# First attention: value products turned over on two column halves, scores two units ahead, probability copies by ScalarE and VectorE in turn

## The chip, the cores and the metric

The kernel runs on one core of one Trainium2 chip. Its engines work from queues of their own and meet in semaphores: TensorE (PE; its weight loads are listed apart as PEld), VectorE (DVE), ScalarE (ACT), GpSimd (POOL) and SyncE (SP), which here issues the loads and stores. The metric is the device time of one execution in microseconds, from start to end of the program; lower is better.

## What is computed

One inference step of a two-layer decoder for 1024 prompt tokens and 8 sample tokens, 1032 columns in all. The change lies in the prompt part of the first layer's latent attention (16 heads):

```python
def mla_prompt_attn(q_nope, q_rope, ckv, k_rope, w_uk, w_uv):
    k_nope = jnp.einsum('nsc,chd->nshd', ckv, w_uk)
    v = jnp.einsum('nsc,chd->nshd', ckv, w_uv)
    ...
    def block(args):
        i, qn_b, qr_b = args
        s = (jnp.einsum('nqhd,nshd->nhqs', qn_b, k_nope)
             + jnp.einsum('nqhr,nsr->nhqs', qr_b, k_rope)).astype(jnp.float32) * MLA_SCALE
        qpos = i * Q_BLOCK + jnp.arange(Q_BLOCK)
        s = jnp.where(kpos[None, :] <= qpos[:, None], s, NEG)
        p = jax.nn.softmax(s, axis=-1).astype(v.dtype)
        return jnp.einsum('nhqs,nshd->nqhd', p, v)
```

A head has 64 plain and 32 rotated query and key columns and 64 value columns. All is float32.

## The kernel before

Activations lie with channels on the partitions and tokens in the columns. The stage is a loop over four groups of four heads (`gi`). In a group TensorE first projects: two tiles of plain queries (L911), a tile of the rotary parts of four heads, keys (L918), the rotary tile with its halves swapped by a product with a permutation matrix (`swap16`, L926), keys again, values (L940). ScalarE and VectorE copy the results out of PSUM and VectorE applies the rotation (L1076 to L1081).

Then come 32 units (`UNITS`): a unit is one head and one block of 128 queries. Causality gives query block `qb` only `qb`+1 key blocks, so units take the blocks in the order 0, 7, 1, 6, 2, 5, 3, 4, each for the two heads of a pair in turn. A unit goes through these steps, each a wait on a semaphore of the step before:

- `scores(u)` on TensorE (L953): queries by up to 1024 keys, into one of two areas of two PSUM banks, by turns.
- `maximum(u)` on VectorE (L1096 to L1098): the causal mask is added to the diagonal block, the row maximum taken and scaled.
- `exponential(u)` on ScalarE (L1022): exp with the row sum beside it, into `prob` in SBUF.
- `turn(u)` on TensorE (L964): the probabilities are transposed block by block, four to a PSUM bank (a batch), by turns into bank 4 and bank 5.
- `turned(u)`: ScalarE copies the even batches out (L1034), VectorE the odd ones (L1119), into `probT`.
- `values(u)` on TensorE (L976): for each key block the transposed probabilities, 128x128, are the stationary side and the 64 value columns of the head stream; the sum is 128 queries by 64.
- `normalise(u)` on VectorE (L1104, L1108): the reciprocal of the row sum, and the product by it, into `onat`.
- `turn_out(pr)` on TensorE (L984) transposes the 128x128 result of a pair of heads, and `outputs(pr)` copies it to `mixa`, on ScalarE (L1041) or VectorE (L1126).

The order on each engine is written out by hand. TensorE's loop over `u` issues `scores(u+1)`, `values(u-1)`, `turn(u)` and, after every second unit, `turn_out`. VectorE's issues `maximum(u+1)`, `normalise(u-1)`, `turned(u)`, `outputs`; ScalarE's `exponential(u+1)`, `turned(u)`, `outputs`. A float32 product is two TensorE instructions in the trace, a transposition one.

After the stage comes decode over the paged cache (L1220 on), whose weights `wukT`, `wuv` and `sel` SP loads behind this stage's weights. Two later places show forms that this stage does not have yet: in decode, products on four 32-column quarters of the array (L1263, L1279), and in the second layer's attention, products on two 64-column halves (L1891) and a lane shuffle on VectorE (L1782).

## Time and profile before

| | us |
|---|---|
| median of 3 runs | 3428.65 |
| lowest and highest | 3427.99, 3432.38 |
| the profiled execution | 3433.76 |
| its span, first to last instruction | 3431.9 |
| TensorE busy in the span | 3109.9 (91%) |
| VectorE busy | 1806.9 (53%) |
| ScalarE busy | 692.1 (20%) |
| GpSimd busy | 881.0 (26%) |
| this stage, first projection to the end of the last output copy | 340.0 to 909.1 |

Durations come from one profiled execution. Matmuls are pipelined, and each is listed with its way through the array, so the pace of a run of matmuls is read from its start to the start of the next, or as the run's length less one tail. In the stage view the columns are the stretch, its length, the busy time and number of instructions of PE, PEld, DVE, ACT and POOL, the granted clock of TensorE as a share of 2.4 GHz, the share of the DMA engines and GB/s. In the timeline they are start, length, engine, line, operation, output and inputs, shapes, number of instructions, and in brackets the idle time before with what ended it.

### The profile page before, as it was taken

What the parts mean: (1) busy time and instruction counts of PE and PEld (TensorE: products, weight loads), DVE (VectorE), ACT (ScalarE), POOL (GpSimd) and SP (SyncE); (2) the same over time, 40 slices, a digit from 0 to 9 for tenths busy, and PEclk for the clock granted to TensorE, in tenths of its full rate; (3) what the DMA queues carried; (4) which work ended last, traced back from release to release, by engine and by line L of the source; (5) the groups of instructions that cost most, each with busy time, mean ns of one, the idle gap of its engine ahead of it and who ended that gap; (6) DMA issues with size and microseconds to landing.
All of it is one profiled execution on the core that took longest, in us unless ns stands there. A gap on an engine that the chain in (4) does not pass through costs nothing. (4 is left out here: it accounts for less than half of the span.)

```text
span 3431.9 us, 58662 instructions
## 1 busy us (share of the span) xinstructions
PE 3109.9 (91%) x21903; PEld 2787.8 (81%) x21903; DVE 1806.9 (53%) x2943; ACT 692.1 (20%) x1446; POOL 881.0 (26%) x496
## 2 busy tenths in 40 slices
PE   6865888888888887999999999998979999999996
PEld 6843666666666666999999999997559999999996
DVE  8694555555455554375253434565865533525354
ACT  3101333333233332021000000100742100000001
POOL 3200000000011111443443434442015344443432
PEclk9887999999899998999999999999989999999998
DMA  2101000100166663111111111122111111111112
GB/s 95 50 1 41 14 1 13 38 0 0 56 194 194 197 192 118 46 55 45 54 43 44 49 43 51 42 64 64 50 53 57 47 43 49 43 49 42 50 42 71
DMA packets 129123, 205.77 MB, mean 60 GB/s; under 512 B 14833, under 2 KB 95729, under 8 KB 128274
## 3 DMA queue, kind: packets, MB, share of 16 engines
q1 hardware_dynamic: 127858, 200.07, 19.1%
q10 hardware_dynamic: 1152, 4.23, 0.3%
q8 instruction: 67, 1.10, 0.1%
q14 instruction: 46, 0.38, 0.0%
HBM read 189.87 MB, written 6.25 MB: 57 GB/s over the span
## 5 line engine op out<-in xcount | busy, mean ns | idle before, releaser
L137 PE MATMUL ps_trunk_out<-sb_h_hi,sb_slab_hi 128*128 128x344 f32 x2400 | 768.0, 320 | 0.0
L138 PE MATMUL ps_trunk_out<-sb_h_hi,sb_slab_lo 128*128 128x344 f32 x2400 | 764.8, 319 | 0.0
L139 PE MATMUL ps_trunk_out<-sb_h_lo,sb_slab_hi 128*128 128x344 f32 x2400 | 764.4, 319 | 0.0
L121 POOL TENSOR_TENSOR sb_slab_hi<-sb_slab_raw,sb_ones 128x1024 fp32r<-128x1024 f32 (+3 forms) x214 | 345.7, 1615 | 1367.0 <-PE ps_trunk_out L139 1051.8
L123 POOL TENSOR_TENSOR sb_slab_lo<-sb_slab_raw,sb_slab_hi 128x1024 fp32r<-128x1024 f32 (+3 forms) x214 | 488.6, 2283 | 16.8
L138 PEld LDWEIGHTS ps_trunk_out<-sb_h_hi,sb_slab_lo 128*128 128x128 f32 x2400 | 450.4, 188 | 0.6
L137 PEld LDWEIGHTS ps_trunk_out<-sb_h_hi,sb_slab_hi 128*128 128x128 f32 x2400 | 450.4, 188 | 0.6
L139 PEld LDWEIGHTS ps_trunk_out<-sb_h_lo,sb_slab_hi 128*128 128x128 f32 x2400 | 450.4, 188 | 0.0
L137 PE MATMUL ps_trunk_out<-sb_ffn_a_hi,sb_slab_hi 128*128 128x344 f32 x1056 | 336.9, 319 | 4.9 <-DVEq L1601 4.9
L139 PE MATMUL ps_trunk_out<-sb_ffn_a_lo,sb_slab_hi 128*128 128x344 f32 x1056 | 337.9, 320 | 0.0
L138 PE MATMUL ps_trunk_out<-sb_ffn_a_hi,sb_slab_lo 128*128 128x344 f32 x1056 | 336.2, 318 | 0.0
L1329 POOL TENSOR_TENSOR sb_dec_kr<-sb_dec_ck,sb_ones 128x256 f32<-128x256 f32 x64 | 46.7, 729 | 1127.6 <-DMA sb_dec_ck<-cache 1030.1
L1554 ACT ACTIVATE sb_ffn_a<-sb_ffn_c 128x1032 f32<-128x1032 f32 x44 | 47.0, 1067 | 995.5 <-DVEq L1591 995.5
L976 PEld LDWEIGHTS ps_mla_bank<-sb_mla_v,sb_mla_probT 128*128 128x128 f32 x1152 | 146.0, 196 | 88.2 <-ACT sb_mla_probT L1034 68.1
L1610 DVE TENSOR_TENSOR sb_z<-sb_z,ps_trunk_out 128x1032 f32 x48 | 59.0, 1229 | 300.5 <-PE ps_trunk_out L139 300.5
L137 PEld LDWEIGHTS ps_trunk_out<-sb_ffn_a_hi,sb_slab_hi 128*128 128x128 f32 x1056 | 198.4, 188 | 6.0 <-DVEq L1601 6.0
L139 PEld LDWEIGHTS ps_trunk_out<-sb_ffn_a_lo,sb_slab_hi 128*128 128x128 f32 x1056 | 198.5, 188 | 0.0
L138 PEld LDWEIGHTS ps_trunk_out<-sb_ffn_a_hi,sb_slab_lo 128*128 128x128 f32 x1056 | 198.4, 188 | 0.0
L976 PE MATMUL ps_mla_bank<-sb_mla_v,sb_mla_probT 128*128 128x64 f32 x1152 | 152.8, 279 | 39.3 <-ACT sb_mla_probT L1034 38.9
L1578 DVE TENSOR_TENSOR sb_ffn_g<-ps_trunk_out,sb_rstd 128x1032 f32<-128x1032 f32 x44 | 54.2, 1233 | 230.6 <-PE ps_trunk_out L139 230.6
L953 PE MATMUL ps_mla_bank<-sb_mla_k,sb_mla_q 96*128 96x512 f32 (+3 forms) x384 | 157.3, 522 | 2.7 <-ACT sb_mla_v L1015 2.7
L1022 ACT ACTIVATE sb_mla_prob<-ps_mla_bank,sb_mla_nmx 128x1024 f32<-128x1024 f32 (+7 forms) x128 | 94.9, 741 | 208.5 <-DVE sb_mla_nmx L1098 191.2
(393 smaller groups left out, 5168.2 us busy)
## 6 DMA issues: line engine op xcount, KB each, us to landing
sb_dec_ck<-cache SPq DMA_DIRECT2D x512, 144.0 KB, 2.4
sb_slab_raw<-f_w_gu SPq DMA_DIRECT2D x88, 512.0 KB, 3.5
sb_slab_raw<-f_w_down SPq DMA_DIRECT2D x32, 384.0 KB, 3.1
sb_slab_raw<-f_w_down SPq DMA_DIRECT2D x32, 320.0 KB, 2.8
sb_slab_raw<-e_w_out SPq DMA_DIRECT2D x24, 256.0 KB, 2.6
sb_slab_raw<-o_w_in SPq DMA_DIRECT2D x12, 512.0 KB, 3.5
sb_slab_raw<-e_w_in SPq DMA_DIRECT2D x10, 512.0 KB, 3.2
sb_x_first<-x SPq DMA_DIRECT2D x8, 516.0 KB, 8.5
```

The source lines that it names most:

```text
L121: nc.gpsimd.tensor_tensor(hi, raw, one, ALU.mult).then_inc(self.hi_done[s], 1)
L123: nc.gpsimd.tensor_tensor(self.lo[:, s, 0:kc, :], raw, hi.bitcast(F32), ALU.subtract).then_inc(self.split_done[s], 1)
L137: nc.tensor.matmul(out[:, t, 0:TT], a, x_hi(k)[:, cols], start=k == 0, stop=False)
L138: nc.tensor.matmul(out[:, t, 0:TT], b, x_hi(k)[:, cols], start=False, stop=False)
L139: last = nc.tensor.matmul(out[:, t, 0:TT], a, x_lo(k)[:, cols], start=False, stop=k == kc - 1)
L953: m = MM(bank[:, 2 * (u % 2) + c0 // 512, 0:c1 - c0], qg[:, h, qb * P:(qb + 1) * P], kg[:, h, c0:c1], start=True, stop=True)
L976: m = MM(bank[:, 6 + u % 2, 0:DV], probT[:, u % 2, kb, :], vg[:, kb, h * DV:(h + 1) * DV], start=kb == 0, stop=kb == qb)
L1022: nc.scalar.activation(prob[:, u % 2, 0:(qb + 1) * P], bank[:, 2 * (u % 2):2 * (u % 2) + 2, :].rearrange("p a b -> p (a b)")[:, 0:(qb + 1) ...
L1329: nc.gpsimd.tensor_tensor(kr[:, c % 2], ck[:, c % SLOTS, :, KVL:CW], one, ALU.mult).then_inc(kr_done, 1)
L1554: nc.scalar.activation(a[:, :], c[:, :], ACT.Gelu_apprx_tanh).then_inc(ffn_act_done, 1)
L1578: ch.link(V.tensor_tensor(v3(g[:, 2:]), slabs.out[:, 0, :, 0:TT], v3(rstd), ALU.mult))
L1610: V.tensor_tensor(xm, xm, slabs.out[:, s, :, 0:TT], ALU.add).then_inc(slabs.free[s], 1)
```

## The change

- Projections: the rotary tile is projected first. The swap of its halves is a `stream_shuffle` on VectorE instead of the product with `swap16`; `ra` and `rb` lie in two tiles of `z`. Key and value projections go to other banks. The decode weights on SP wait until VectorE has ended the fourth group's projections.
- Units: four units form a quad: small block, large block, for head 0, then the same for head 1 ((0,7), (1,6), (2,5), (3,4)). Small scores have bank 4, large ones banks 0 and 1 or 2 and 3. `prob` and `probT` are doubled.
- TensorE issues `scores(u+2)`, `turn(u)`, and, twice per quad, `values(pr)` for a pair of heads: the value columns are stationary and the transposed probabilities stream, head 0 on array columns 0 to 63 and head 1 on 64 to 127. The result is already turned. A second product, ones by `diag`, spreads the inverse row sums over the partitions.
- VectorE takes one reciprocal per pair; GpSimd makes `diag`, the identity times the inverse sums. `outputs` on VectorE copies the spread sums to `over` and multiplies the result by them into `mixa`. `normalise`, `turn_out` and the copies after it go.
- Batches are numbered so that a large unit's two batches go to ScalarE and VectorE one each, and the small units' by turns.

```diff
+            prob = [sb("mla_prob_s", [P, 2, 512]), sb("mla_prob_l", [P, 2, T])]
+            probT = [sb("mla_probT_s", [P, 2, 2, 4, P]), sb("mla_probT_l", [P, 2, 2, QB, P])]
+            mx, nmx = sb("mla_mx", [P, 4]), sb("mla_nmx", [P, 4])
+            rs, rinv, diag = sb("mla_rs", [P, 2, 4]), sb("mla_rinv", [P, 4]), sb("mla_diag", [P, 2, 2, P])
+            over = sb("mla_over", [P, 1, P])
...
+            def unit(u):
+                qd, big, hh = u // 4, u % 2, u // 2 % 2
+                qb = ((0, 7), (1, 6), (2, 5), (3, 4))[qd % 4][big]
+                return qd, big, hh, qb, 2 * (qd // 4) + hh
+            def batches(u):
+                qd, big, hh, qb, _ = unit(u)
+                b = 6 * qd + 3 * hh + big
+                return [(b + j, 4 * j, min(4, qb + 1 - 4 * j)) for j in range(1 + big)]
+            def score(u):
+                _, big, hh, qb, _ = unit(u)
+                s = bank[:, 2 * hh:2 * hh + 2, :].rearrange("p a b -> p (a b)") if big else bank[:, 4, :]
+                return s[:, 0:(qb + 1) * P]
...
+                    sp.wait_ge(dve_ev, 4 * 5)
                     sp.dma_start(wukT[:, :, :], A["w_ukT"]).then_inc(dec_w_in, 16)
...
+                @block.gpsimd
+                def _(pool):
+                    with pool.Fori(0, 4) as gi:
+                        for pr in range(NPAIR):
+                            big = pr % 2
+                            pool.wait_ge(rinv_done, gi * NPAIR + (pr + 1))
+                            nc.gpsimd.tensor_tensor(diag[:, big], ident[:, :].unsqueeze(1).broadcast_to((P, 2, P)),
+                                                    rinv[:, 2 * big:2 * big + 2].unsqueeze(2).broadcast_to((P, 2, P)),
+                                                    ALU.mult).then_inc(diag_done, 1)
...
+                        pe.wait_ge(w_in, gi * 32 + 32)
+                        pe.wait_ge(exp_done, gi * UNITS + 1)
+                        queries(2, 0)
+                        for e in t_ev:
+                            pe.wait_ge(e, gi * (NB // 2) + 1)
+                        queries(0, 3)
+                        pe.wait_ge(act_ev, gi * 5 + 1)
+                        queries(1, 0)
+                        pe.wait_ge(o_done, gi * NPAIR + 1)
+                        keys(0, 6)
...
-                        for t in range(3):
-                            m = MM(bank[:, t, 0:TT], swap16[:, :], qraw[:, t * TT:(t + 1) * TT], start=True, stop=True)
-                        m.then_inc(proj, 1)
...
+                        keys(1, 3)
+                        for v, b0 in enumerate((5, 6, 7, 0)):
...
+                        def scores(u):
+                            qd, big, hh, qb, h = unit(u)
+                            if big and u >= 4:
+                                pe.wait_ge(exp_done, gi * UNITS + (u - 2))
+                            elif not big and u >= 2:
+                                pe.wait_ge(exp_done, gi * UNITS + u)
+                            for c0 in range(0, (qb + 1) * P, 512):
+                                c1 = min((qb + 1) * P, c0 + 512)
+                                m = MM(score(u)[:, c0:c1], qg[:, h, qb * P:(qb + 1) * P], kg[:, h, c0:c1], start=True, stop=True)
...
+                        def turn(u):
+                            qd, big, hh, qb, h = unit(u)
+                            pe.wait_ge(exp_done, gi * UNITS + (u + 2))
+                            for b, b0, nb in batches(u):
+                                if b >= 2:
+                                    pe.wait_ge(t_ev[b % 2], gi * (NB // 2) + (b // 2 + 1))
+                                for q in range(nb):
+                                    m = nc.tensor.transpose(bank[:, 5 + b % 2, q * P:(q + 1) * P],
+                                                            prob[big][:, hh, (b0 + q) * P:(b0 + q + 1) * P], ident[:, :])
+                                m.then_inc(t_done, 1)
+                        def values(pr):
+                            u = last_of(pr)
+                            qd, big, _, qb, h = unit(u)
+                            for e in range(2):
+                                pe.wait_ge(t_ev[e], gi * (NB // 2) + (3 * qd + (4 if big else 2 + e)))
+                            pe.wait_ge(o_done, gi * NPAIR + (pr + 1))
+                            for kb in range(qb + 1):
+                                for hh in range(2):
+                                    MM(bank[hh * DV:(hh + 1) * DV, 7, big * 256:big * 256 + P],
+                                       vg[:, kb, (h - 1 + hh) * DV:(h + hh) * DV], probT[big][:, qd % 2, hh, kb, :],
+                                       start=kb == 0, stop=kb == qb)
+                            pe.wait_ge(diag_done, gi * NPAIR + (pr + 1))
+                            for hh in range(2):
+                                m = MM(bank[hh * DV:(hh + 1) * DV, 7, big * 256 + P:big * 256 + 2 * P], ones[:, 0:DV],
+                                       diag[:, big, hh, :], start=True, stop=True)
+                            m.then_inc(pv_done, 1)
+                        pe.wait_ge(act_ev, gi * 5 + 3)
+                        scores(0)
...
-                        for u in range(UNITS + 2):
-                            if u + 1 < UNITS:
-                                scores(u + 1)
-                            if 1 <= u <= UNITS:
-                                values(u - 1)
+                        for u in range(UNITS + 1):
+                            if u + 2 < UNITS:
+                                scores(u + 2)
                             if u < UNITS:
                                 turn(u)
-                            if u >= 3 and u % 2 == 1:
-                                turn_out((u - 3) // 2)
+                            if u >= 3 and u % 4 in (3, 0):
+                                values((u - 3) // 4 * 2 + (u % 4 == 0))
...
+                            if u >= 4:
+                                act.wait_ge(t_done, gi * NB + (batches(u - 4)[-1][0] + 1))
+                            nc.scalar.activation(prob[big][:, hh, 0:(qb + 1) * P], score(u), ACT.Exp, scale=MLA_SCALE,
+                                                 bias=nmx[:, u % 4:u % 4 + 1],
+                                                 accum_out=rs[:, qd % 2, 2 * big + hh:2 * big + hh + 1]).then_inc(exp_done, 1)
...
                                 act.wait_ge(t_done, gi * NB + (b + 1))
-                                nc.scalar.copy(mixa[:, bass.ds(gi * 2 + hp, 1), qb * P:(qb + 1) * P],
-                                               bank[:, 4:5, 0:P]).then_inc(ta_ev, 1)
+                                nc.scalar.copy(probT[big][:, qd % 2, hh, b0:b0 + nb, :],
+                                               bank[:, 5 + b % 2, 0:nb * P].rearrange("p (a b) -> p a b", b=P)).then_inc(t_ev[0], 1)
...
+                        dve.wait_ge(act_ev, gi * 5 + 1)
+                        V.tensor_tensor(ra, qraw[:, :], rot[:, 0, :], ALU.mult)
+                        ch.link(V.stream_shuffle(rb, qraw[:, :], swap_lanes))
+                        ch.link(V.tensor_tensor(rb, rb, rot[:, 1, :], ALU.mult))
...
+                        def inverse(pr):
+                            big = pr % 2
+                            dve.wait_ge(exp_done, gi * UNITS + (last_of(pr) + 2))
+                            V.reciprocal(rinv[:, 2 * big:2 * big + 2],
+                                         rs[:, pr // 2 % 2, 2 * big:2 * big + 2]).then_inc(rinv_done, 1)
...
+                                if b % 2:
+                                    dve.wait_ge(t_done, gi * NB + (b + 1))
+                                    V.tensor_copy(probT[big][:, qd % 2, hh, b0:b0 + nb, :],
+                                                  bank[:, 6, 0:nb * P].rearrange("p (a b) -> p a b", b=P)).then_inc(t_ev[1], 1)
+                        def outputs(pr):
+                            qd, big, _, qb, _ = unit(last_of(pr))
+                            dve.wait_ge(pv_done, gi * NPAIR + (pr + 1))
+                            ch.link(V.tensor_copy(over[:, 0, :], bank[:, 7, big * 256 + P:big * 256 + 2 * P]))
+                            V.tensor_tensor(mixa[:, bass.ds(gi * 2 + qd // 4, 1), qb * P:(qb + 1) * P],
+                                            bank[:, 7:8, big * 256:big * 256 + P], over[:, :, :], ALU.mult).then_inc(o_done, 1)
...
-                            if u + 1 < UNITS:
-                                maximum(u + 1)
-                            if 1 <= u <= UNITS:
-                                normalise(u - 1)
+                            if u >= 4 and u % 4 in (0, 1):
+                                outputs((u - 4) // 4 * 2 + u % 4)
+                            if u + 2 < UNITS:
+                                maximum(u + 2)
+                            if u < UNITS and u % 4 >= 2:
+                                inverse(u // 4 * 2 + u % 4 - 2)
                             if u < UNITS:
                                 turned(u)
-                            if u >= 3 and u % 2 == 1:
-                                outputs((u - 3) // 2)
```

## Rows read from the trace of the kernel before

**Rows 1.** The page's head.

```profile
span 3431.9 us, 58662 instructions
```

**Rows 2.** Stages: length, busy PE, PEld, DVE, ACT, POOL; granted clock.

```profile
340.00:909.10 569.10, 495.71 (x2608) 353.14 (x2608) 305.66 (x820) 187.03 (x415) 0.00 (x0) 0.95 0.03 10
...
481.80:517.80 36.00, 33.59 (x108) 21.11 (x108) 13.74 (x13) 6.24 (x7) 0.00 (x0) 0.95 0.00 0
...
935.00:1320.00 385.00, 337.61 (x4590) 258.81 (x4590) 220.34 (x642) 144.84 (x412) 45.20 (x62) 0.99 0.64 184
...
2436.00:2533.00 97.00, 86.52 (x598) 53.05 (x598) 82.39 (x250) 65.48 (x247) 0.00 (x0) 1.00 0.17 55
```

**Rows 3.** Waits from 377 to 909 us: total us, times, longest.

```profile
PE ps_mla_bank L976 <- ACT sb_mla_probT L1034: 38.9, 52, 2.1
...
PE ps_mla_bank L984 <- ACT sb_mla_probT L1034: 15.3, 30, 0.7
...
DVE sb_mla_onat L1108 <- PE ps_mla_bank L976: 44.0, 56, 2.3
```

**Rows 4.** Timeline of group 1: start us, length, engine, what.

```profile
418.77 1.45 PE L976 MATMUL ps_mla_bank<-sb_mla_v,sb_mla_probT 128*128 128x64 f32 x12
...
418.98 0.30 DVE L1096 TENSOR_TENSOR ps_mla_bank<-ps_mla_bank,sb_mla_mask 128x128 f32<-128x128 f32 x1 [1.31 <-PE ps_mla_bank L953]
...
433.25 1.88 PE L953 MATMUL ps_mla_bank<-sb_mla_k,sb_mla_q 96*128 96x512 f32 x4
...
434.92 1.11 ACT L1022 ACTIVATE sb_mla_prob<-ps_mla_bank,sb_mla_nmx 128x1024 f32<-128x1024 f32 x1 [3.37 <-DVE sb_mla_nmx L1098]
...
436.50 0.91 PEld L964 LDWEIGHTS ps_mla_bank<-sb_ident,sb_mla_prob 128*128 128x128 f32 x8
```

**Rows 5.** VectorE's groups by shape, 377 to 909 us: busy, mean, idle.

```profile
L1096 DVE TENSOR_TENSOR ps_mla_bank<-ps_mla_bank,sb_mla_mask 128x128 f32<-128x128 f32 x128 | 38.1, 297 | 81.9 <-PE ps_mla_bank L953 81.2
...
L1108 DVE TENSOR_SCALAR sb_mla_onat<-ps_mla_bank,sb_mla_rinv 128x64 f32<-128x64 f32 x128 | 36.3, 284 | 63.6 <-PE ps_mla_bank L976 44.0 <-issue 14.2
...
L1098 DVE TENSOR_SCALAR sb_mla_nmx<-sb_mla_mx 128x1 f32<-128x1 f32 x128 | 19.6, 153 | 4.4
...
L1097 DVE TENSOR_REDUCE sb_mla_mx<-ps_mla_bank 128x1 f32<-128x1024 f32 x16 | 19.6, 1224 | 0.5
...
L1097 DVE TENSOR_REDUCE sb_mla_mx<-ps_mla_bank 128x1 f32<-128x128 f32 x16 | 4.7, 291 | 0.5
...
L1119 DVE COPY sb_mla_probT<-ps_mla_bank 128x512 f32<-128x512 f32 x24 | 16.5, 690 | 7.2 <-PE ps_mla_bank L964 5.9
```

**Rows 6.** Timeline of the second layer's attention: products on two column halves.

```profile
2445.79 0.63 PEld L1891 LDWEIGHTS ps_swa_bank<-sb_swa_probT,sb_swa_v 128*64 128x64 f32 x8 [0.17 <-issue]
...
2446.80 0.30 PEld L1866 LDWEIGHTS ps_swa_bank<-sb_swa_mask_r,sb_ident_r 128*128 128x128 f32 x2 [0.39 <-issue]
```

**Rows 7.** Timeline of decode, weight loads: four column quarters.

```profile
1119.27 0.30 PEld L1260 LDWEIGHTS ps_dec_bank<-sb_dec_kT,sb_dec_qd 128*128 128x128 f32 x2 [0.41 <-issue]
...
1119.69 0.40 PEld L1263 LDWEIGHTS ps_dec_bank<-sb_dec_cT,sb_dec_qc 128*32 128x32 f32 x16
...
1120.28 0.20 PEld L1246 LDWEIGHTS ps_dec_bank<-sb_ident,sb_dec_kr 128*128 128x128 f32 x2 [0.20 <-issue]
```

**Rows 8.** Timeline of the decode stage, GpSimd beside VectorE.

```profile
1138.87 0.73 POOL L1329 TENSOR_TENSOR sb_dec_kr<-sb_dec_ck,sb_ones 128x256 f32<-128x256 f32 x1 [5.83 <-DMA sb_dec_ck<-cache]
...
1138.96 0.66 DVE L1420 TENSOR_TENSOR sb_dec_mnew<-sb_dec_cmax,sb_dec_m 128x1 f32<-128x1 f32 x1
```

**Rows 9.** Timeline of group 2's projections, TensorE.

```profile
502.62 1.90 PE L926 MATMUL ps_mla_bank<-sb_mla_qraw,sb_swap 128*128 128x344 f32 x6
...
505.33 3.70 PE L918 MATMUL ps_mla_bank<-sb_z,sb_mla_wkv 128*128 128x512 f32 x8 [0.81 <-DVE sb_mla_k L1073]
...
513.42 3.72 PE L940 MATMUL ps_mla_bank<-sb_mla_wkv,sb_z 128*128 128x256 f32 x16 [0.93 <-DVE sb_mla_v L1085]
```

**Rows 10.** VectorE's groups by line, whole span: the shuffle.

```profile
L1782 DVE STREAM_SHUFFLE sb_swa_zs<-sb_z 128x1032 f32<-128x1032 f32 x10 | 13.4, 1340 | 0.1
```

More of the change, by code:

```diff
@@ L901, in _, with queries @@
                     with pe.Fori(0, 4) as gi:
-                        pe.wait_ge(w_in, gi * 32 + 32)
-                        for e in (ta_ev, td_ev):
-                            pe.wait_ge(e, gi * (NB // 2) + 1)
-                        for tile, b0, (s, w) in ((0, 0, (None, 0)), (1, 3, (None, 0)), (2, 0, (act_ev, 1))):
-                            if s is not None:
-                                pe.wait_ge(s, gi * 5 + w)
+                        def queries(tile, b0):
                             for t in range(3):
@@ L946, in scores @@
                         def scores(u):
-                            hp, qb, hh = units[u]
-                            h, n = 2 * hp + hh, (qb + 1) * P
-                            if u >= 2:
-                                pe.wait_ge(exp_done, gi * UNITS + (u - 1))
-                            for c0 in range(0, n, 512):
-                                c1 = min(n, c0 + 512)
-                                m = MM(bank[:, 2 * (u % 2) + c0 // 512, 0:c1 - c0], qg[:, h, qb * P:(qb + 1) * P],
-                                       kg[:, h, c0:c1], start=True, stop=True)
+                            qd, big, hh, qb, h = unit(u)
@@ L987, in _ @@
-                        scores(0)
-                        for u in range(UNITS + 2):
-                            if u + 1 < UNITS:
-                                scores(u + 1)
-                            if 1 <= u <= UNITS:
-                                values(u - 1)
+                        pe.wait_ge(act_ev, gi * 5 + 3)
+                        scores(0)
+                        pe.wait_ge(act_ev, gi * 5 + 5)
+                        scores(1)
+                        pe.wait_ge(dve_ev, gi * 5 + 5)
@@ L1012, in _ @@
                         m.then_inc(act_ev, 1)
-                        for v in (1, 3):
-                            act.wait_ge(proj, gi * NPROJ + (8 + v))
-                            nc.scalar.copy(vg[:, 2 * v:2 * v + 2, :], v2(bank[:, 7, :])).then_inc(act_ev, 1)
+                        for v, b0 in ((1, 6), (3, 0)):
+                            act.wait_ge(proj, gi * NPROJ + (7 + v))
+                            nc.scalar.copy(vg[:, 2 * v:2 * v + 2, :], split2(bank[:, b0, :])).then_inc(act_ev, 1)
@@ L1037, in outputs @@
-                        def outputs(pr):
-                            (hp, qb, _), b = units[2 * pr], of_pair(pr)
-                            if b % 2 == 0:
+                            if u >= 4:
[3 more added lines that the diff above has]
+                                                 accum_out=rs[:, qd % 2, 2 * big + hh:2 * big + hh + 1]).then_inc(exp_done, 1)
@@ L1044, in _ @@
                         exponential(0)
-                        for u in range(UNITS + 2):
+                        for u in range(UNITS):
                             if u + 1 < UNITS:
                                 exponential(u + 1)
-                            if u < UNITS:
-                                turned(u)
-                            if u >= 3 and u % 2 == 1:
-                                outputs((u - 3) // 2)
+                            turned(u)
                 @block.vector
@@ new lines, in _ @@
+                        m.then_inc(dve_ev, 1)
+                        dve.wait_ge(proj, gi * NPROJ + 5)
+                        for hh in range(2):
+                            m = V.tensor_copy(split2(kg[0:NOPE, hh, :]), bank[hh * NOPE:(hh + 1) * NOPE, 6:8, :])
+                        m.then_inc(dve_ev, 1)
+                        for v, b0 in ((0, 5), (2, 7)):
+                            dve.wait_ge(proj, gi * NPROJ + (7 + v))
+                            V.tensor_copy(vg[:, 2 * v:2 * v + 2, :], split2(bank[:, b0, :])).then_inc(dve_ev, 1)
@@ new lines, in maximum @@
+                        def maximum(u):
+                            qd, big, hh, qb, _ = unit(u)
+                            s, c = score(u), slice(u % 4, u % 4 + 1)
+                            block_ = s[:, qb * P:(qb + 1) * P]
+                            dve.wait_ge(s_done, gi * UNITS + (u + 1))
+                            ch.link(V.tensor_tensor(block_, block_, mask[:, 1, :], ALU.add))
+                            ch.link(V.tensor_reduce(mx[:, c], s, AX, ALU.max))
+                            V.tensor_scalar(nmx[:, c], mx[:, c], -MLA_SCALE, None, ALU.mult).then_inc(mx_done, 1)
@@ L1087, in _ @@
+                        maximum(0)
+                        dve.wait_ge(act_ev, gi * 5 + 2)
                         dve.wait_ge(dve_ev, gi * 5 + 5)
                         V.tensor_copy(qs[:, bass.ds(gi * HG, HG), :], qg[:, :, T:NT]).then_inc(qs_done, 1)
-                        def maximum(u):
-                            hp, qb, hh = units[u]
-                            s = bank[:, 2 * (u % 2):2 * (u % 2) + 2, :].rearrange("p a b -> p (a b)")
-                            diag = s[:, qb * P:(qb + 1) * P]
-                            c = slice(u % 4, u % 4 + 1)
-                            dve.wait_ge(s_done, gi * UNITS + (u + 1))
-                            ch.link(V.tensor_tensor(diag, diag, mask[:, 1, :], ALU.add))
-                            ch.link(V.tensor_reduce(mx[:, c], s[:, 0:(qb + 1) * P], AX, ALU.max))
-                            V.tensor_scalar(nmx[:, c], mx[:, c], -MLA_SCALE, None, ALU.mult).then_inc(mx_done, 1)
```

160 lines of the change are left out of this document (38 added, 122 removed).

## The prediction

> **What bounds the kernel now.** I read the stage view first. The diff touches one stage, the first layer's prompt attention, which runs from 340.0 to 909.1 us of a span of 3431.9 us [rows 1, 2]: 569.1 us, four equal groups of 142.3 us, each with 36.0 us of projections and 106.3 us of attention. TensorE is the engine to look at: 495.7 of 569.1 us busy against 305.7 on VectorE and 187.0 on ScalarE. A busy TensorE is not a full one, so I read the pace from the timeline. At the full 2.4 GHz a score product of 1024 keys (four instructions) takes 1.88 us with its tail, so 0.213 us per 128 keys; twelve instructions of the value products take 1.45 us, so 0.119 us each; eight transposes load in 0.91 us, so 0.117 us each with the step to the next [rows 4]. One group has 144 key blocks (each of four heads has 36), so scores cost 144 x 0.213 = 30.7 us, transposes 144 x 0.117 = 16.9 us, values 288 instructions x 0.119 = 34.3 us, and the 16 transposes of outputs 1.9 us: 83.8 us of the 106.3. The rest is in the wait view: TensorE stands before the value products and before the output transposes for ScalarE's copies, 38.9 + 15.3 us, with smaller ones about 66 us over the four groups, or 16.5 per group [rows 3]. 83.8 + 16.5 is 100.3; the granted clock of 0.95 over the stage [rows 2] (a tenth of the time at 1.2 GHz) makes up the other 5 or so. So the stage is TensorE's own pace plus a round trip through the other engines in each unit.
>
> **The value products.** Now the transposed probabilities (128 columns) are the stationary side and 64 value columns stream; the weight load sets the 0.119 us. After, 64 value columns are stationary and the probabilities stream, 128 columns, with heads 0 and 1 of a pair on the two column halves. Instructions per key block stay two. What one costs depends on whether the halves run side by side. Rows of such products stand in this trace: in the second layer eight instructions of 256 columns on two halves take 1.01 us from first load to the next line's first load, 0.17 us of it a gap, so 0.107 us each, half of the 0.213 us that 256 columns take alone [rows 4, 6]. In decode sixteen of 128 columns on four quarters need 0.59 us with 0.20 us of gap, 0.025 us each, a quarter [rows 7]. Mine are 128 columns on two halves: 0.107/2 = 0.053, taken as 0.055 us. Bounds: 0.053 from below, 0.107 (no overlap) from above; I take the low end because both neighbours overlap fully. Each block of value products also switches the array twice. The rows show 0.17 us going in and 0.2 to 0.4 us of loader idling going out, 0.17 us of it lost [rows 6, 7]; I charge 0.30 us per block.
>
> The Trainium skill, "TensorEngine Tiling (Array Packing)", Key Properties, says that changing the tiling mode drains the engine; it gives no figure. The gaps of rows 6 and 7 agree. By a reading without that rule the sum would be 16 x 0.30 x 4 = 19 us lower.
>
> **The division.** The row scaling (128 x 284 ns on VectorE [rows 5]), 64 output transposes and the 64 copies after them go. In their place, per pair of heads: one reciprocal instead of two, a GpSimd product of 128x256, four TensorE instructions that spread the inverse sums (0.22 us), and on VectorE a copy and a product of 128x128 out of PSUM, 0.29 and 0.30 us by the nearest forms [rows 5], 0.65 us with the step between. A block for n key blocks on TensorE is then V(n) = 0.22n + 0.52 us. The GpSimd product is 0.73 us for the same size [rows 8]; it starts at least 1.5 us before TensorE asks for it, so it costs nothing; it would have to take about 3 us to count. Beside such a product VectorE's operation of one column on two SBUF tensors took 0.66 us [rows 8] (0.15 us for a one-column operation with no product beside it [rows 5]); the loop has no VectorE operation with two SBUF tensors, so I charge 0 (upper bound: 0.5 us x 64 = 32 us).
>
> **The order.** Scores are now issued two units ahead, small and large query blocks alternate with three score areas, so TensorE no longer waits for the maximum and exponential of the unit just scored. Per quad (two blocks, two heads, nine key blocks per head) TensorE's work is 3.84 (scores) + 2.1 (transposes) + 0.22 x 9 + 1.04 (values) = 9.0 us, VectorE's about 8.3 us: 4 x (0.30 + 0.15) masks and scalings, 3.03 reductions, 1.67 copies, 1.3 outputs, steps. Both nearly equal, so I walked the queues of one quad with these prices: M(n) = 0.67 + 0.133n for a maximum (from the two reductions, 291 and 1224 ns), 0.69 us for a copy of four blocks, 1.1 us + 0.1 for the widest exponential, 0.2 us from a product to its reader (the next line's matmul starts at 418.77, the mask addition at 418.98) [rows 4, 5]. Two stalls stay. (a) The first half of head 0's large transposes is copied by VectorE, but queued behind the maximum of the next large unit; the next small unit's transposes need that buffer. With the end of the large score product at 0, the maximum ends at 0.2 + 1.74, the copy at 2.62; TensorE has work only until 1.36: 1.3 us lost. (b) The large block's value products wait for the copy of the second half, behind another maximum, and for the small block's outputs: 7.57 us against 6.62 us, 0.9 us lost. The walk for the four kinds of quad, us from the end of the current large scores:
>
> | blocks, then next | first-half copy | small transposes | next large scores | large transposes | small values | second copy | outputs | large values | end |
> |---|---|---|---|---|---|---|---|---|---|
> | 1+8, 2+7 | 2.62 | 2.8 | 4.3 | 5.2 | 6.0 | 6.9 | 7.5 | 9.85 | 11.3 |
> | 2+7, 3+6 | 2.49 | 2.8 | 4.05 | 4.9 | 5.8 | 6.4 | 7.0 | 9.1 | 10.4 |
> | 3+6, 4+5 | 2.36 | 2.8 | 3.8 | 4.5 | 5.7 | 6.1 | 6.7 | 8.9 | 9.9 |
> | 4+5, 1+8 | 2.22 | 2.7 | 4.4 | 5.0 | 6.4 | 6.8 | 7.4 | 9.1 | 10.8 |
>
> Each column ends where its engine and its wait allow. Seven steps from quad to quad sum to 74.2 us. The start costs 5.2 us: small score 0.2, value copy 0.6, large 1.7, small 0.2, large 1.7, and 0.5 as the second maximum is still running. The end is 7.7 us: 3.8 until the last transpose, 1.4 and 1.6 for the values, 0.9 for the outputs between them. Attention is 87.1 us per group at full clock, against 100.3 by the same prices now.
>
> **The projections.** The swap product goes, 1.72 us per group (1.90 with its tail), and a shuffle of 1.34 us on VectorE comes [rows 9, 10]. The rotary tile comes first, so the 8.7 us of VectorE's rotary work run under the next two query tiles (2 x 5.16 us); VectorE is free for its copies at 15.7 us, when the third tile is ready. Keys and values get other banks: the waits of 0.81 + 0.93 us (1.0 + 1.1 at the loader) go [rows 9], and the last shrinks by 0.5. 36.0 - 1.7 - 2.1 - 0.5 = 31.7 us; 0.6 of that last wait is already in the 5.2 above, so 31.1. If VectorE is late there, up to the same 2.1 us comes back. The three weight loads for decode now wait until VectorE has ended group 4's projections, some 85 us before decode reads them; nothing but they are queued behind that on SP. Cost 0. ScalarE keeps its load within a few us and waits most of the time.
>
> **The sum.** Per group 31.1 + 87.1 = 118.2 us; for TensorE's share at the lower clock I add 3.5 us to the attention (4.5% of its 72 us; the projections' 36.0 holds its own): 121.7. Four groups and 0.9 us for the last outputs: 487.7 against 569.1 us, 81.4 less. The profiled execution took 3433.8 us; 3352.4 is its forecast. The median of the runs is 3428.65, 5.1 us lower, so I predict 3347.3 us.
>
> **The rivals.**
> - The two stalls vanish, because VectorE's queue turns faster than I walked it (its copies overlap by 0.08 us each) and TensorE runs at its own pace: 1.6 us x 32 quads = 51 us more, 3296. For it: the engines' sums allow it. Against: the copy behind the maximum is in program order, and that chain has no slack. 0.10.
> - VectorE becomes the bound: each of its steps waits longer than walked, 1.5 us more per quad, 48 us: 3395. For it: 8.3 of 10.6 us of a quad is VectorE work, and all four chains cross it. 0.14. The Trainium skill's same page, PSUM Bottleneck, warns that a faster array leaves the copies out of PSUM as the limit; its reading is this rival, and the VectorE sum above agrees that it is near.
> - The halves do not overlap with 128 streaming columns: 0.107 instead of 0.055 us. After what the stalls hide, 13.6 us per group return, 54 in all: 3401. Rows 6 and 7 speak against it. 0.08.
> - The change does not do what it says: the scores are not ahead in effect, TensorE still waits 16.5 us per group; what stays is 83.8 - 71.9 (9.0 x 8) = 11.9 us and the projections' 4.3, 65 us: 3364, inside the main case.
> - Slower: the granted clock. If half-array products with the stalls between let the clock fall to 1.2 GHz, TensorE's 72 us of attention per group take twice that at worst: +288 us, 3635. It turns the sign once a further 28% of that work runs at the low level. Against: the clock was 0.99 in decode and 1.00 in the second layer's attention, both with column tiles [rows 2]; stalls here are of the length of those now. 0.04.
> - Same as before within 0.2% (which is about what a measurement of this kernel can tell from no change): several of these at once. 0.02.
>
> **How the numbers follow.** Forecast 0.62, 3347.3, its own range 3322 to 3375 (stall prices off by a third either way, and the 0.5 us per GpSimd product as far as it would fall on the path). The range wanted holds eight in ten: from 3305, short of the first rival, to 3398, which takes in the VectorE rival and most of the shared-port bound. Faster by over 0.2%: 0.94; within: 0.02; slower: 0.04.
>
> **What would show it.** Stage about 488 us. L1096's mask additions start 0.2 us after the score products, with TensorE idle mainly before small units' transposes and before the large block's value products, released by VectorE copies. Value product loads 0.055 us apart. Head 0's first-half copy of a large unit follows the maximum. GpSimd busy about 47 us more, no wait on it. I am wrong if the value instructions stand 0.1 us apart, if the clock in the stage falls under 0.9, or if the idle time ahead of the transposes is absent or double.

## The result and the profile after

The changed kernel takes 3338.18 us (median of 4 runs, 3337.84 to 3343.56); the kernel before takes 3428.32 us beside it. The ratio is 0.9742, with a 95% interval of 0.9729 to 0.9756: 2.6% faster. The forecast was 3347.3 us, 9.1 us too slow, inside its own narrow range of 3322 to 3375.

First the page's head after and the lines that answer to the table of before: TensorE is busy 75 us less, VectorE 7 us and ScalarE 9 us less, GpSimd 39 us more.

```profile
span 3336.0 us, 58640 instructions
## 1 busy us (share of the span) xinstructions
PE 3034.9 (91%) x22071; PEld 2720.9 (82%) x22071; DVE 1800.3 (54%) x2855; ACT 682.9 (20%) x1414; POOL 920.4 (28%) x560
```

The stage view of after, the answer to [rows 2]: group 1, group 2's projections and the stage; group 2's attention stands with the experiment on the look-ahead (length, busy PE, PEld, DVE, ACT, POOL, then the granted clock as the third number from the end).

```profile
339.70:459.90 120.20, 107.79 (x695) 72.56 (x695) 73.77 (x181) 45.02 (x96) 9.80 (x16) 0.96 0.03 10
459.90:489.40 29.50, 29.50 (x105) 19.56 (x104) 15.47 (x16) 5.64 (x6) 0.00 (x0) 1.00 0.00 1
...
339.70:812.40 472.70, 420.12 (x2776) 284.22 (x2776) 296.84 (x732) 178.31 (x383) 39.19 (x64) 0.98 0.04 12
```

The stage went from 569.1 to 472.7 us, 96.4 less; the span fell by 95.9, so all of the gain is here. TensorE starts a group's projections at 339.7, 459.9, 576.4 and 692.9 us, so the groups take 120.2, 116.5, 116.5 and 119.5 us, against 142.3 before. In group 2, 29.5 us are projections, with TensorE busy throughout, where they were 36.0. Group 1's projections follow a wait of 13.0 us for the weights and have a granted clock of 0.91, those of the other groups 1.00.

The waits of after in the stage, the answer to [rows 3] (engine, line, releaser: total us, times, longest; PE first, then its loader, then VectorE):

```profile
PE ps_mla_bank L976 <- DVE sb_mla_probT_l L1109: 34.6, 32, 1.6
...
PE ps_mla_bank L988 <- DVE sb_mixa L1116: 9.9, 15, 0.8
PE ps_mla_bank L976 <- ACT sb_mla_prob_l L1034: 4.1, 4, 1.0
...
PEld ps_mla_bank L988 <- DVE sb_mixa L1116: 15.7, 24, 1.2
...
DVE ps_mla_bank L1092 <- PE ps_mla_bank L966: 50.9, 64, 1.3
```

The old waits for ScalarE's copies, 38.9 + 15.3 us, are gone. In their place stand the two stalls of the forecast: 32 waits of 1.08 us (one in each of 32 quads) before a small unit's transposes, released by VectorE's first-half copy (a), and a shorter one before the large block's value products, released by VectorE's outputs (b).

One quad in the timeline of after (start us, length, engine, line, what). It shows the turned-over products and both stalls.

```profile
384.33 0.29 DVE L1116 TENSOR_TENSOR sb_mixa<-ps_mla_bank,sb_mla_over 128x128 f32 x1 [0.16 <-DVE sb_mla_over L1115]
...
384.68 1.73 PEld L988 LDWEIGHTS ps_mla_bank<-sb_mla_probT_l,sb_mla_v 128*64 128x64 f32 x32 [0.94 <-DVE sb_mixa L1116]
...
386.37 0.25 PEld L993 LDWEIGHTS ps_mla_bank<-sb_mla_diag,sb_ones 128*64 128x64 f32 x4
...
386.80 0.30 PEld L966 LDWEIGHTS ps_mla_bank<-sb_mla_k,sb_mla_q 96*128 96x128 f32 x2 [0.17 <-issue]
386.80 1.77 PE L966 MATMUL ps_mla_bank<-sb_mla_k,sb_mla_q 96*128 96x512 f32 x4
...
388.61 0.30 DVE L1092 TENSOR_TENSOR ps_mla_bank<-ps_mla_bank,sb_mla_mask 128x128 f32<-128x128 f32 x1 [0.95 <-PE ps_mla_bank L966]
388.94 1.09 DVE L1093 TENSOR_REDUCE sb_mla_mx<-ps_mla_bank 128x1 f32<-128x896 f32 x1
...
390.16 0.69 DVE L1109 COPY sb_mla_probT_l<-ps_mla_bank 128x512 f32<-128x512 f32 x1
...
391.00 0.41 PE L976 MATMUL ps_mla_bank<-sb_ident,sb_mla_prob_s 128*128 128x128 f32 x2 [1.02 <-DVE sb_mla_probT_l L1109]
```

The 32 loads of the large block run from 384.68 to the next line's first load at 386.37, 0.053 us apart: the pace at which two halves side by side had been priced. The array's switch is the gap of 0.17 us ahead of L966. Stall (a) is in the last four lines: all transposes of the large unit have been in PSUM since 389.3, but VectorE first does the mask (388.61) and the maximum (388.94) of the next large unit, copies at 390.16, and TensorE starts its next transposes at 391.00.

### The profile page after: what moved, and what is told of

The parts are those of the page before. It is cut to its first block and busy times, and to the rows that moved or that the text cites. A ratio compares the mean times of both kernels' runs of the same rounds, so it can differ in the third digit from the quotient of the medians.

```text
span 3336.0 us, 58640 instructions
## 1 busy us (share of the span) xinstructions
PE 3034.9 (91%) x22071; PEld 2720.9 (82%) x22071; DVE 1800.3 (54%) x2855; ACT 682.9 (20%) x1414; POOL 920.4 (28%) x560
## 5 line engine op out<-in xcount | busy, mean ns | idle before, releaser
L913 POOL TENSOR_TENSOR sb_mla_diag<-sb_ident,sb_mla_rinv 128x256 f32<-128x256 f32 x64 | 39.2, 612 | 632.3 <-DVE sb_mla_rinv L1099 632.3
L966 PE MATMUL ps_mla_bank<-sb_mla_k,sb_mla_q 96*128 96x512 f32 (+3 forms) x384 | 150.7, 503 | 1.8 <-ACT sb_mla_v L1027 1.8
L1235 PE MATMUL ps_dec_bank<-sb_ident,sb_dec_ck 128*128 128x128 f32 x1024 | 134.3, 275 | 0.0
L1582 DVE TENSOR_TENSOR sb_ffn_u<-sb_rstd,ps_trunk_out 128x1032 f32<-128x1032 f32 x44 | 54.1, 1230 | 135.3 <-PE ps_trunk_out L139 135.0
```

Source lines behind the costliest of these rows:

```text
L966: m = MM(score(u)[:, c0:c1], qg[:, h, qb * P:(qb + 1) * P], kg[:, h, c0:c1], start=True, stop=True)
L1235: m = nc.tensor.transpose(bank[:, b % 4, k * P:(k + 1) * P], src, ident[:, :])
L1582: ch.link(V.tensor_tensor(v3(u[:, :]), v3(rstd), slabs.out[:, 1, :, 0:TT], ALU.mult))
```

## The experiments

All have the changed kernel as their base, and each ratio is to the kernel before on the same chip. The runs of before scatter by up to 7 us either way, so I read differences from the changed kernel's 3338.2 us in medians, beside the ratio. Where a few us matter I compare the attention of one group at a granted clock of 1.00 in both kernels: it is 87.0 us in the changed kernel (group 2).

**Do the halves run side by side?**

```diff
-for kb in range(qb + 1):
-    for hh in range(2):
+for hh in range(2):
+    for kb in range(qb + 1):
         MM(bank[hh * DV:(hh + 1) * DV, 7, ...
```

> Head 1's value products come after all of head 0's, each still on its own column half, so no two neighbours lie on different halves. Same instructions, same count. Theory (the halves run side by side): a value load stands 0.107 instead of 0.053 us from the next, and 54 us come back: about 3392 us. Rival (a 64-column load alone gives the pace of 0.053 us, neighbours don't matter): unchanged, 3338 us.

3372.47 us, ratio 0.9823 (0.9807 to 0.984): 34 us slower. Its loads in the same large block:

```profile
384.28 2.87 PEld L988 LDWEIGHTS ps_mla_bank<-sb_mla_probT_l,sb_mla_v 128*64 128x64 f32 x30 [0.94 <-DVE sb_mixa L1116]
```

30 loads in 2.87 us, the last one's own 0.14 us taken off, are 0.094 us apart; the same reading of the changed kernel (1.73 us, 32 loads) gives 0.051. The same instructions on the same halves, only in another order, take 1.8 times as long, so the pace comes from neighbours on different halves. The rival of an unchanged time falls. The size was wrong, 34 us where the expectation had 54: a load takes 0.094, not 0.107 us, the change of heads inside a block keeps its short step, and with one key block the order of heads changes nothing (four loads of 0.20 us in both). The stalls did not hide any of it: the sums of the two waits are the same 34.6 and 10.0 us, and TensorE's idle time in group 2's attention is 13.0 us against 13.1.

**Stall (a): is it the copy's place in VectorE's queue?** The first kernel moves one copy per quad to ScalarE (the edit below, shortened; each copy still raises the semaphore of its batch), the second moves them all.

```diff
 for b, b0, nb in batches(u):      # ScalarE
-    if b % 2:
+    if b % 2 and b % 6 != 1:
         continue
...
-    if b % 2:                     # VectorE
+    if b % 2 and b % 6 != 1:
```

> One copy per quad moved from VectorE to ScalarE: the first half of head 0's large transposes, the one that stands behind the maximum (stall a). Theory (this queue position is what TensorE waits for): the 34.6 us of TensorE's waits for it go, and VectorE has 0.69 us less to do in each of 32 quads: 30 to 42 us faster than the changed kernel, about 3300 us. Rival (the sum of VectorE's work is what bounds, and only its 22 us less count): about 3316 us. Rival (the wait only moves to the next one): 3333 to 3338 us.

> All copies of transposed probabilities on ScalarE, none on VectorE. Theory (both stalls come from copies queued behind a maximum on VectorE): the walk of a quad with 1+8 blocks gives 9.6 instead of 11.3 us; over 32 quads about 48 us less than the changed kernel, 3290 us. Rival (ScalarE, with exponentials and all copies in one queue, becomes the late one): the stall of the first half is replaced by one before the transposes, 3320 us or more.

The first took 3307.68 us, ratio 0.9635 (0.9619 to 0.9652): 30.5 us faster than the changed kernel. All copies on ScalarE took 3297.62 us, ratio 0.9615 (0.9599 to 0.9631): 40.6 us faster. TensorE's waits of the first, then of the second (same view as above):

```profile
PE ps_mla_bank L988 <- DVE sb_mixa L1116: 9.0, 16, 0.8
PE ps_mla_bank L976 <- ACT sb_mla_prob_l L1034: 7.7, 12, 1.0
PE ps_mla_bank L976 <- ACT sb_mla_probT_l L1046: 4.4, 8, 0.7
```

```profile
PE ps_mla_bank L976 <- ACT sb_mla_prob_l L1034: 6.5, 8, 1.0
PE ps_mla_bank L988 <- DVE sb_mixa L1114: 4.5, 8, 0.8
PE ps_mla_bank L976 <- ACT sb_mla_probT_l L1044: 4.4, 8, 0.7
```

Moving one copy of 0.69 us takes 34.6 us of waits down to 4.4 and leaves (b) nearly as it was; 3.6 us move to the waits for the exponential (4.1 to 7.7). 30.5 us come off the time. At a clock of 1.00 the attention of a group falls from 87.0 to 79.9 us, 28.6 us over four groups; the other 2 us are no more than the clock costs the changed kernel in the attention of groups 1 and 4 (3 us). VectorE's whole queue as the bound would have given 22. Moving the rest halves (b) and gives 10 us more. The two stalls together are worth 41 us where the walk had 48 to 51. ScalarE has room: in group 2 of the second kernel it is busy 52.8 us of 107.5. The Trainium skill, "TensorEngine Tiling (Array Packing)", PSUM Bottleneck, advises the use of both ScalarE and VectorE to empty PSUM; by that the changed kernel's split should be the better one. Here the measurement decides against it by 41 us: VectorE's queue also holds the maxima, and a copy behind one holds up TensorE. This version beats both kernels.

**What the look-ahead is worth.**

```diff
-if u + 2 < UNITS:
-    scores(u + 2)       # VectorE: maximum(u + 2)
+if u + 1 < UNITS:
+    scores(u + 1)       # VectorE: maximum(u + 1)
```

> Scores and maximum are issued only one unit ahead instead of two; all else as changed. Theory (the look-ahead is what hides the chain score, maximum, exponential): a large unit's chain is 0.2 + 1.7 + 1.1 = 3.0 us, the TensorE work behind it about 1 us, so up to 2 us per large unit, 128 in all, less what the present stalls already hold (up to 70): 3400 to 3470 us. Rival (as in the prediction, the scores not being ahead costs only the old waits): about 3364 us or less.

3426.97 us, ratio 0.9989 (0.9975 to 1.0003). One unit less of look-ahead gives back 89 us, nearly the whole gain, and the time is inside the first theory's range. The rival, which is the prediction's "the scores are not ahead in effect", falls: it had 3364. The waits, and the stage view of group 2's attention in this kernel and in the changed one:

```profile
PE ps_mla_bank L976 <- ACT sb_mla_prob_l L1033: 73.7, 40, 2.7
```

```profile
510.56:623.82 113.26, 92.56 (x593) 62.14 (x591) 60.07 (x167) 37.83 (x90) 9.80 (x16) 0.82 0.03 10
```

```profile
489.40:576.42 87.02, 73.90 (x594) 50.43 (x592) 58.70 (x167) 39.21 (x90) 9.80 (x16) 1.00 0.04 13
```

Of the 26.2 us that this attention is longer, TensorE's idle time is only 7.6 (20.7 against 13.1). The other 18.7 is busy time for the same instructions: the granted clock stands at 0.82 instead of 1.00 (0.85 or 0.86 in the other three groups), so part of them ran at 1.2 GHz. Over the four attentions idle time grows by 32 us and busy time by 59. My expectation had only waits, up to 2 us for each large unit, so its range was met for the wrong reason.

**Stall (b): are VectorE's outputs on the path?**

```diff
-ch.link(V.tensor_copy(over[:, 0, :], bank[:, 7, big * 256 + P:big * 256 + 2 * P]))
...
-    bank[:, 7:8, big * 256:big * 256 + P], over[:, :, :], ALU.mult)
+    bank[:, 7:8, big * 256:big * 256 + P], ones[:, :].unsqueeze(1), ALU.mult)
```

> Leaves out VectorE's copy of the spread inverse sums, and with it the division: the output product multiplies by ones. 64 copies of 0.29 us and the step of 0.16 us behind each go from VectorE; TensorE does all it did. Theory (stall b: the large block's value products wait for the small block's outputs): 0.45 us per quad, 14 us faster than the changed kernel, 3324 us. Rival (VectorE's whole queue is the bound): 0.45 us x 64 = 29 us faster, 3309 us. Rival (the outputs are off the path): 3338 us.

3326.77 us, ratio 0.9702 (0.9686 to 0.9718): 11.4 us faster, nearest to the 14 us of the first theory. The wait of stall (b), 9.9 us in the changed kernel, is now:

```profile
PE ps_mla_bank L988 <- DVE sb_mixa L1115: 4.0, 12, 0.5
```

The small block's outputs are on the path once per quad; VectorE's sum is not the bound (29 us), and they are not off the path either.

**GpSimd's product: how long may it take?** The next two kernels widen it (the cut edit below; VectorE's reciprocal writes its two values three times for it); the second also runs it twice in a chain.

```diff
-nc.gpsimd.tensor_tensor(diag[:, big], ... (P, 2, P) ..., ALU.mult).then_inc(diag_done, 1)
+nc.gpsimd.tensor_tensor(diag[:, big], ... (P, 6, P) ..., ALU.mult).then_inc(diag_done, 1)
```

> GpSimd's product is three times as wide (128x768 instead of 128x256; TensorE reads the first third), so at most 1.84 us instead of 0.61. Theory (hidden: in the changed kernel TensorE asks 1.3 us after it in a small block and 2.3 us after it in a large one): within 5 us of the changed kernel, 3338. Rival (a longer GpSimd product holds up VectorE, as the one-column operation of 0.66 us seemed to say): 0.2 to 0.5 us per product, 13 to 32 us slower, 3351 to 3370 us, with VectorE's operations visibly longer.

> Two such wide products one after the other, at most 3.7 us. Theory (the slack is 1.3 us in small blocks and 2.3 in large ones, so 1.9 and 2.9 us are the longest that stay hidden): 1.8 us late in a small and 0.8 us in a large block, 26 to 83 us slower over 32 quads, 3364 to 3421 us, and TensorE waits for GpSimd before the four products of the sums. Rival (slack is larger than it looks): 3338 us.

The single wide product took 3338.30 us, ratio 0.9734 (0.9718 to 0.9751), the two in a chain 3370.68 us, ratio 0.9827 (0.9811 to 0.9843). Groups by shape of the single wide product, then one wait of the double one:

```profile
L913 POOL TENSOR_TENSOR sb_mla_diag<-sb_ident,sb_mla_rinv 128x768 f32<-128x768 f32 x64 | 94.1, 1471 | 580.1 <-DVE sb_mla_rinv L1099 579.9
L1092 DVE TENSOR_TENSOR ps_mla_bank<-ps_mla_bank,sb_mla_mask 128x128 f32<-128x128 f32 x128 | 37.9, 296 | 51.8 <-PE ps_mla_bank L966 50.8
L1094 DVE TENSOR_SCALAR sb_mla_nmx<-sb_mla_mx 128x1 f32<-128x1 f32 x128 | 19.6, 153 | 4.4
```

```profile
PE ps_mla_bank L997 <- POOL sb_mla_diag L917: 30.7, 35, 1.2
```

1.47 us cost nothing, and VectorE's masks and scalings keep their mean of 296 and 153 ns (297 and 153 before, [rows 5]). Two such products, 3.0 us, cost 32 us and make 30.7 us of waits, nearly all in the small blocks: 1.1 us late in each of 32 by a limit of 1.9 us is 35. The range was met only because it was wide; I had taken 1.84 us for a product, where it is 1.47. No VectorE operation in this loop has two inputs in SBUF, so what such a one would lose beside GpSimd is not tried here.

**What a switch of the array's mode costs.** One more product between the value products and those of the sums, on the full array or on one half:

```diff
+MM(bank[:, 7, big * 256 + P:big * 256 + 2 * P], ident[:, :], ident[:, :], ...)      # full array
...
+MM(bank[0:DV, 7, big * 256 + P:big * 256 + 2 * P], ident[:, 0:DV], ident[:, :], ...)  # one half
```

> One more full-array product (identity by identity, 128 columns, two instructions) between the value products and the products of the sums, so two more switches of the array's mode per block, 128 in all; its result is overwritten. Theory (a switch costs the 0.17 us gap each way): 64 x (0.21 + 0.34) = 35 us slower, 3373 us. Rival (switches are free, the gaps are something else): 64 x 0.21 = 13 us, 3351 us.

> The same extra product (two instructions, 128 columns) but on one column half, between products that lie on column halves too: no further switch. Theory: 64 x 0.11 to 0.21 = 7 to 14 us slower than the changed kernel, 3345 to 3352 us, and about 22 us faster than the kernel with the full-array product. Rival (the switches are free): both kernels within 7 us of each other.

The full-array product took 3367.32 us, ratio 0.9817 (0.9801 to 0.9833), the half-array one 3352.50 us, ratio 0.9775 (0.9759 to 0.9792): 29 and 14 us over the changed kernel. The large block's loads, full array first:

```profile
383.49 1.73 PEld L988 LDWEIGHTS ps_mla_bank<-sb_mla_probT_l,sb_mla_v 128*64 128x64 f32 x32 [0.37 <-DVE sb_mixa L1117]
385.39 0.30 PEld L991 LDWEIGHTS ps_mla_bank<-sb_ident 128*128 128x128 f32 x2 [0.17 <-issue]
385.80 0.20 PEld L994 LDWEIGHTS ps_mla_bank<-sb_mla_diag,sb_ones 128*64 128x64 f32 x4
386.17 0.30 PEld L966 LDWEIGHTS ps_mla_bank<-sb_mla_k,sb_mla_q 96*128 96x128 f32 x2 [0.17 <-issue]
```

```profile
385.22 1.73 PEld L988 LDWEIGHTS ps_mla_bank<-sb_mla_probT_l,sb_mla_v 128*64 128x64 f32 x32 [0.73 <-DVE sb_mixa L1117]
386.91 0.25 PEld L991 LDWEIGHTS ps_mla_bank<-sb_ident 128*64 128x64 f32 x2
387.02 0.35 PEld L994 LDWEIGHTS ps_mla_bank<-sb_mla_diag,sb_ones 128*64 128x64 f32 x4
387.55 0.30 PEld L966 LDWEIGHTS ps_mla_bank<-sb_mla_k,sb_mla_q 96*128 96x128 f32 x2 [0.17 <-issue]
```

From the first load of L988 to the first of L966 the block takes 2.68 us with the full-array product, 2.33 with the half-array one and 2.12 in the changed kernel (384.68 to 386.80). So the product costs 0.21 us either way, and two switches 0.35 us on top, 0.17 each: the gap is the cost. The expectations had 35 us for the first kernel, 7 to 14 for the second and 22 between them. In the medians only 15 of those 22 show. The wait for VectorE ahead of the block shrinks (0.37 us against 0.73): a group's attention at a clock of 1.00 is 94.8 us against 89.8, 20 us over four groups. Some 2 us more are the clock, for which the half-array kernel paid 6 us (two groups at 0.97 and 0.95) and the other 4 (0.98 and 0.96); the last 3 us are within the scatter of the medians. The rival of free switches, within 7 us, falls.

**Do TensorE's waits bring the clock down?** GpSimd's wide product three times in a chain.

> Three of the wide GpSimd products in a chain (one takes 1.47 us, so 4.5 us; TensorE reads the last): 2.6 us late in a small and 1.6 us in a large block by the slack of 1.9 and 2.9 us. The question is TensorE's clock. With one unit of look-ahead TensorE waited up to 2.7 us at a time and its clock in the attention was 0.82; with two products here it waited up to 1.2 us more and the clock held 0.99. Theory (waits of more than 2 us in each quad bring the clock down): waits of 4.2 us per quad make 134 us, some of it in place of the present stalls (70), and a clock near 0.85 adds some 50 us: 3450 to 3510 us. Rival (the clock holds at 0.97 or more, what brought it down was something else in that kernel): 3400 to 3470 us, and products of values keep 0.053 us in each block.

3493.37 us, ratio 1.0188 (1.0169 to 1.0207), inside the first theory's range and outside the rival's. Group 2's attention with two such products, and with three:

```profile
496.87:592.91 96.04, 77.29 (x594) 51.28 (x592) 59.81 (x168) 39.47 (x90) 46.75 (x32) 0.98 0.03 12
```

```profile
525.25:651.51 126.26, 95.37 (x593) 63.60 (x591) 59.73 (x167) 39.30 (x90) 70.23 (x48) 0.82 0.03 9
```

```profile
PE ps_mla_bank L1001 <- POOL sb_mla_diag L921: 83.4, 41, 2.7
```

TensorE does the same work in both. With waits of up to 1.2 us for GpSimd and 1.6 us for VectorE the clock is 0.98 in this group and 1.00 in the other three; with waits of up to 2.7 us it is 0.82 (0.86 in group 1), as with one unit of look-ahead, though scores are two ahead here. Against the changed kernel this attention is 39.2 us longer: 17.8 idle and 21.5 busy. With two products at a clock of 1.00 TensorE was busy 76.0 us, 2.1 more than in the changed kernel, so some 19 of the 21.5 are the clock. Over four groups that is 73 us idle and 78 busy, where the theory had priced the clock at 50.

It is not TensorE's idle time in total: with one unit of look-ahead a group's attention has 20.7 us of it at a clock of 0.82, with two GpSimd products 19.7 us at 1.00. What the two kernels at 0.82 share is single waits of up to 2.7 us in each quad. Where between these kernels the clock starts to fall, no run shows, and such waits are not all there is to it: single groups stood at 0.95 to 0.98 with the same waits as their neighbours at 1.00, as in the half-array kernel above.

## Why the prediction was right, point by point

- **What bounds the stage.** Right. TensorE's pace and the round trip through the others were the two parts, and undoing either half of the cure costs: 34 us for the overlap of halves, 89 us for the look-ahead.
- **Value products, 0.055 us each.** Right: 0.053. The upper bound, no overlap, was somewhat too dear: 0.094 instead of 0.107 us, so its rival at 3401 would have come out near 3372.
- **The switches, 0.30 us per block.** 0.34 by the rows and the two runs with an extra product. The block of eight key blocks takes 0.17 + 2.12 = 2.29 us, and V(8) was 2.28.
- **The division.** Right that GpSimd's product hides, at 0.61 us, and right that VectorE has nothing to lose beside it. The step "it would have to take about 3 us to count" was wrong: it was read from the large blocks. TensorE asks earlier in the small ones, which count from 1.9 us; a product of 3.0 us cost 32 us.
- **The order and the two stalls.** The large scores of successive quads in group 1 end at 376.89, 388.57, 398.89, 408.92 and 419.60 us, so quads take 11.7, 10.3, 10.0 and 10.7 us; the walk had 11.3, 10.4, 9.9 and 10.8. Group 2's attention is 87.0 us at a granted clock of 1.00; the walk had 87.1 at full clock. Inside the quad the stalls are smaller than priced (1.08 instead of 1.3 us for (a), 0.3 to 0.5 by 9.9 and 15.7 us over 32 quads instead of 0.9 for (b)), and TensorE's own work is a little more (73.9 us busy in group 2 against 72). The walk's seven steps also add up to 74.0 us and not 74.2. That these cancel is luck; which copy and which queue make the stall is shown by moving that copy.
- **The projections.** Right. The 31.1 us held about 1.9 us for the clock (the three query tiles took 17.4 us before, 3 x 5.16 = 15.5 at full clock); without it the forecast is 29.2, and 29.5 came.
- **The sum.** Without the clock a group was 29.2 + 87.1 = 116.3 us; groups 2 and 3 took 116.5. The one step that failed is "for TensorE's share at the lower clock I add 3.5 us", with the 1.9 us kept in the projections: 5.4 us per group, 21.6 in all. (4.5% of 72 us is 3.2, not 3.5; that slip is 1 us in all.) Groups 2 and 3 paid none of it. Groups 1 and 4 took 3.7 and 3.0 us more than these, 0.9 of it the last outputs that the sum has apart, so the clock cost 5.8 in all. The 15.8 us between, less 0.2 us per group, are the whole miss of the stage, 487.7 against 472.7 us. I took the clock of before as a property of the stage, where it moves with TensorE's waits: the last experiment shows that longer waits of TensorE bring it down. Whether the old waits of up to 2.1 us were what lowered it to 0.95 before [rows 2, 3] was not tried by itself.
- **From execution to median.** The profiled execution came out 14.6 us under its forecast (3337.84 against 3352.4 us), the median only 9.1, since the profiled execution of after lies at the median and that of before lay 5 us above.
- **The rivals.** "The stalls vanish", 3296 us, describes no run of this kernel, and the version with all copies on ScalarE took 3297.6. That the two agree is luck: the rival took 51 us off a forecast that was 9 us too high, and the version took 41 off. VectorE as the bound is refuted by the two kernels that lighten it: its 22 and 29 us were 30.5, from one copy's place, and 11.4, from one of two outputs. The halves overlap. "The scores are not ahead" was priced at 3364 by keeping the old waits; the run took 3427, since in the new order the whole chain of score, maximum and exponential of a large unit stands open, and the clock falls with it. A slower kernel through the clock did not come, but the mechanism is real: three GpSimd products made the kernel 1.9% slower than before, and about half of its 155 us over the changed kernel is the clock.
- **Decode's weight loads.** Cost 0, as said: from the start of decode to the end of the span it is 2523.0 us (812.97 to 3336.0) against 2522.2 (909.73 to 3431.9).

## What to carry to other kernels

When two engines share a queue of copies, look at what each copy stands behind, not at the engines' sums: one copy of 0.69 us behind a maximum cost 30 us, and giving it to the engine that mostly waits was worth a third of the whole change. Walk one period of the queues with durations from the trace; here it gave each quad to 0.4 us, though the stalls inside it came out smaller than walked. Don't carry the clock of the old kernel into the forecast of the new one: ask how long TensorE's longest regular waits will be.

## What the runs showed of the hardware

- In the two kernels with TensorE waits of up to 2.7 us in each quad the granted clock of the attention was 0.82 to 0.86, where it is 0.98 to 1.00 in the changed kernel. The clock cost as much as the waits or more: some 19 us beside 17.8 in group 2 with three GpSimd products, up to 18.7 beside 7.6 with one unit of look-ahead. With waits of up to 1.6 us for VectorE and 1.2 us for GpSimd in each quad it was 1.00 in three groups and 0.98 in one.
- Loads of 64 columns for products on alternating halves stand 0.051 to 0.053 us apart, one after the other on the same half 0.094 us.
- A switch of the array between halves and whole costs 0.17 us each way: two more switches made a block 0.35 us longer.
- GpSimd's product of two SBUF tensors took 0.61 us for 256 columns and 1.47 us for 768, so, by a line through these two, 0.43 us per 256 columns and about 0.2 us fixed.
